# Matrix-memory mixer: the two halves of the partitions both filled with chunks, narrow products alternated over the array, and two pairs of output banks

## What is computed

```python
def step(carry, inp):                       # one chunk of 64 tokens, each head and direction
    c_mat, n_vec, m = carry
    qb, kb, vb, li, lf = inp
    b = jnp.cumsum(lf, -1)
    dmat = jnp.where(tri, b[..., :, None] - b[..., None, :] + li[..., None, :], -jnp.inf)
    m_inter = b + m[..., None]
    m_t = jnp.maximum(m_inter, jnp.max(dmat, -1))
    s = jnp.einsum('zhtd,zhsd->zhts', qb, kb) * jnp.exp(dmat - m_t[..., None])
    inter = jnp.exp(m_inter - m_t)
    num = inter[..., None] * jnp.einsum('zhtd,zhde->zhte', qb, c_mat) + jnp.einsum('zhts,zhse->zhte', s, vb)
    den = inter * jnp.einsum('zhtd,zhd->zht', qb, n_vec) + jnp.sum(s, -1)
    h_out = num / jnp.maximum(jnp.abs(den), jnp.exp(-m_t))[..., None]
    b_last = b[..., -1]
    g = b_last[..., None] - b + li
    m_new = jnp.maximum(b_last + m, jnp.max(g, -1))
    wts, decay = jnp.exp(g - m_new[..., None]), jnp.exp(b_last + m - m_new)
    c_mat = decay[..., None, None] * c_mat + jnp.einsum('zhs,zhsd,zhse->zhde', wts, kb, vb)
    n_vec = decay[..., None] * n_vec + jnp.einsum('zhs,zhsd->zhd', wts, kb)
    return (c_mat, n_vec, m_new), h_out
```

## Time and profile before

| what | value |
|---|---|
| three executions | 2066.82, 2070.66, 2060.62 us; median 2066.82 us |
| span of the profiled execution | 2063.7 us; its own time is not listed apart from the three |
| PE busy | 1966.4 us, 95% of the span |
| DVE, ACT, POOL busy | 732.5, 407.5, 39.4 us |
| DMA | 512.93 MB, mean 249 GB/s |
| chain that ended last | PE 87%, DMA 5%, DVE 4%, issue 2%, ACT 2% |

### The profile page before, as it was taken

How to read it: one execution, slowest core, us unless ns; L and a number is a source line. 1 busy time by engine, 2 the same in 40 slices (tenths; PEclk the granted TensorE clock), 3 DMA queues, 4 the chain that set the end, 5 groups by cost and what they waited for, 6 DMA issues and landing times.

```text
span 2063.7 us, 34642 instructions
## 1 busy us (share of the span) xinstructions
PE 1966.4 (95%) x15286; PEld 1321.4 (64%) x15286; DVE 732.5 (35%) x1578; ACT 407.5 (20%) x804; POOL 39.4 (2%) x41
## 2 busy tenths in 40 slices
PE   6999988999999999999899999999998989999998
PEld 3554865887554455445475888888877876463564
DVE  2694589564311111111335255323673420010001
ACT  3200263322211111111235200003222120000001
POOL 0000211000000000000000000000000000000000
PEclk9999997799999999999999999999999999999999
DMA  9710006017799999999756369753300059999992
GB/s 366 255 41 0 1 1 229 20 42 285 302 430 426 429 428 427 426 431 429 291 220 245 132 226 376 275 206 131 126 19 2 1 225 361 413 409 407 412 401 97
DMA packets 162338, 512.93 MB, mean 249 GB/s; under 512 B 9070, under 2 KB 32413, under 8 KB 149533
## 3 DMA queue, kind: packets, MB, share of 16 engines
q1 hardware_dynamic: 146720, 481.18, 59.0%
q10 hardware_dynamic: 15485, 29.77, 3.9%
HBM read 509.88 MB, written 1.05 MB: 248 GB/s over the span
## 4 chain that ended last, share of the span: by engine, by line
PE 87%; DMA 5%; DVE 4%; issue 2%; ACT 2%; SPq 0%; DVEq 0%; POOL 0%; ACTq 0%; POOLq 0%
PE PS L389 26%; PE PS L2614 11%; PE PS L2638 5%; PE PS L2450 4%; PE PS L2529 3%; PE PS L2740 3%; PE PS L2540 3%; PE PS L2732 3%; DMA work<-in_moe_w_gate_up_dram 2%; PE PS L396 2%; DMA work<-in_w_ada_dram 2%; PE PS L3324 2%; PE PS L2744 2%; PE PS L2820 1%; PE PS L2159 1%
## 5 line engine op out<-in xcount | busy, mean ns | idle before, releaser
L389 PE MATMUL PS<-hT,work 128*128 128x256 f32 x1408 | 313.1, 382 | 0.0
L389 PEld LDWEIGHTS PS<-hT,work 128*128 128x128 f32 x1408 | 266.8, 191 | 42.2 <-issue 6.2
L2614 PE MATMUL PS<-work,sq 128*64 128x512 f32 x1024 | 222.6, 592 | 0.0
L389 PE MATMUL PS<-work 128*128 128x256 f32 (+1 forms) x544 | 177.1, 486 | 0.0
L2614 PEld LDWEIGHTS PS<-work,sq 128*64 128x64 f32 x1024 | 76.6, 137 | 143.2 <-issue 142.4
L389 PEld LDWEIGHTS PS<-work 128*128 128x128 f32 x544 | 103.0, 190 | 73.5 <-issue 66.0
L2638 PE MATMUL PS<-work 128*64 128x512 f32 x512 | 113.4, 595 | 10.1 <-issue 8.7
L2638 PEld LDWEIGHTS PS<-work 128*64 128x64 f32 x512 | 36.8, 137 | 76.4 <-issue 74.5
L2732 PE MATMUL PS<-work,sq 128*64 128x512 f32 (+1 forms) x384 | 78.8, 568 | 5.6 <-DMA work<-in_moe_w_gate_up_dram 5.6
L2682 DVE TENSOR_TENSOR work<-work,PS 128x64 f32<-128x64 f32 x128 | 18.2, 213 | 184.9 <-PE PS L2614 184.9
L2450 PE MATMUL PS<-work 128*128 128x256 f32 x352 | 76.3, 379 | 0.0
(11 more groups left out here) (662 smaller groups left out, 2628.9 us busy)
## 6 DMA issues: line engine op xcount, KB each, us to landing
work<-in_ex_gate_dram SPq DMA_DIRECT2D x32, 2048.0 KB, 12.6
work<-in_ex_up_dram SPq DMA_DIRECT2D x32, 2048.0 KB, 15.3
work<-in_ex_down_dram SPq DMA_DIRECT2D x32, 2048.0 KB, 11.4
work<-in_moe_w_gate_up_dram SPq DMA_DIRECT2D x32, 2048.0 KB, 13.3
work<-in_moe_w_down_dram SPq DMA_DIRECT2D x16, 2048.0 KB, 16.4
work<-in_ada_w_dram ACTq DMA_DIRECT2D x14, 2048.0 KB, 11.1
work<-in_moe_w_gate_up_dram SPq DMA_DIRECT2D x16, 1536.0 KB, 14.9
work<-in_ada_w_dram SPq DMA_DIRECT2D x10, 2048.0 KB, 11.0
```

The costliest lines, as they stand in the source:

```text
L389: ins = pe.matmul(outp, lhs, rhs, start=n == 0, stop=n == len(pairs) - 1, **kw)
L2614: ins = pe.matmul(PS[pair[m], 6 + j, :], xs[:, k, pair[m]], unit(U[name] + 3 * m + j, KT, F)[:, k, :], start=k == 0, stop=k == KT - 1)
```

## The change

Pairs of chunks (`cp`, 128 tokens) take the place of single chunks, on all 128 partitions: gate tokens, values, keys, decays, scores. Consecutive products go to different quarters or halves of PE's array by their partitions. The state keeps only the wanted blocks (even heads in the lower, odd heads in the upper partitions), so `Cst` is half as wide and needs no zeros. The two directions of a step always have chunks of opposite parity, so their outputs stand in opposite halves of one pair of banks, and successive steps take turns between banks 0, 1 and 2, 3; the state products take turns between banks 6, 7 and 4, 5. PE does the states of the next steps ahead of the outputs. In an output group PE waits once for its own records of the crossed products (`ml_num`, 2j + 1), as they go into the same places from other rows of the array. DVE gets eight small copies that bring floors and decays into the new order (`ml_floors_dve`). Waits elsewhere get new numbers only.

The core of the diff; lines of bodies that only lose are left out, they are in the listing above:

```diff
-    wtok = gates.take(NCH, R40)
-    gtok = gates.take(2, 4, R40)
+    wtok = gates.take(4, R40)
+    btok = gates.take(2, R40)
+    floors = gates.take(4, H)
+    decq = gates.take(4, 2, 4)
+    diag = gates.take(4, R40)
+    den, rden = gates.take(H), gates.take(H)
-    diag = ml.take(4, R40)
-    decb = ml.take(4, R40)
-    vt = ml.take(NCH, H, E1)
-    Cst = ml.take(4, 2, 8 * E1).rearrange("p j d (b q h e) -> p j d b q h e", b=2, q=2, h=2)
+    vt = ml.take(4, H, E1)
+    Cst = ml.take(4, 2, 4 * E1)
-    kwl = ml.take(2, 3, H * C)
-    Em = ml.take(8, H, C)
-    hs = ml.take(4, H * C)
-    den, rden = ml.take(H), ml.take(H)
+    kwl = ml.take(2, 2, H * C)
+    Em = ml.take(2, 2, H * C).rearrange("p c d (h t) -> p c d h t", t=C)
+    hs = ml.take(2, H * C)
...
-        pool.memset(vt[0:C, :, :, C:E1], 1.0)
-        pool.memset(Cst.rearrange("p j d b q h e -> p (j d b q h e)"), 0.0)
+        pool.memset(vt[:, :, :, C:E1], 1.0)
...
+        for g, (t, t0, n) in enumerate(((a_, N, 2), (wts, 0, 4), (einvm, 0, 2))):
+            for cp in range(n):
+                at = ML_SMALL[g] + cp * R40
+                pe.transpose(PS[:, 3, at:at + R40], t[0:R40, t0 + cp * P:t0 + (cp + 1) * P], i40)
...
         for d, rows in enumerate((nD, b_)):
-            if d:
-                pe.wait_ge(S["gate_rows"], 1)
-            for b in range(4):
-                for k in range(2):
-                    ins = pe.matmul(PS[0:C, 4 * (1 - d) + b, k * N:(k + 1) * N], pick[:, d * H + 2 * b + k, :], rows[:, N:],
-                                    start=True, stop=True)
+            by_half = rows[:, N:].rearrange("p (c r t) -> p r c t", r=2, t=C)
+            for b in range(2):
+                for k in range(4):
+                    for r in range(2):
+                        ins = pe.matmul(PS[half(r), 4 + 2 * d + b, k * P:(k + 1) * P].rearrange("p (c t) -> p c t", t=C),
+                                        pick[:, d * H + 4 * b + k, :], by_half[:, r], start=True, stop=True)
                 ins.then_inc(S["ml_e"], 1)
...
+        dve.tensor_copy(btok, ml_small(0, 2))
+        dve.tensor_copy(wtok, ml_small(1, 4)).then_inc(S["gate_rows"], 1)
...
+    def ml_floors_dve():
+
+        for r in range(2):
+            for d in range(2):
+                at = slice(3 - r, None, -2) if d else slice(r, None, 2)
+                dve.tensor_copy(floors[half(r), at, :].rearrange("p c (b q) -> p c b q", b=2),
+                                ml_small(2, 2)[half(r), :, gate_rows[d]].rearrange("p c (q b) -> p c b q", b=2))
+        for b in range(2):
+            for d in range(2):
+                at = slice(None, None, -1) if d else slice(None)
+                ins = dve.tensor_copy(decq[both(b), at, d, :],
+                                      ml_small(3, 4)[both(b), :, gate_rows[d]].rearrange("p c (q b) -> p b c q", b=2)[:, b])
+        ins.then_inc(S["gate_rows"], 1)
...
+        def turn(cp):
+            if cp >= 2:
+                pe.wait_ge(S["ml_kw"], cp - 1)
             for p in range(4):
+                ins = pe.transpose(PS[:, cp % 2, p * P:(p + 1) * P], k1[:, p, cp * P:(cp + 1) * P], ident)
             ins.then_inc(S["keys_turned"], 1)
         turn(0)
         turn(1)
+        for cp in range(4):
+            pe.wait_ge(S["gate_rows"], 1 + cp + 1)
+            for p in range(4):
+                ins = pe.transpose(PS[:, 4 + cp, p * P:(p + 1) * P], mv[:, p, cp * P:(cp + 1) * P], ident)
+            ins.then_inc(S["ml_vt"], 1)
+        pe.wait_ge(S["gate_rows"], 6)
+        for cp in range(2):
+            for h in range(H):
+                for c in (2 * cp, 2 * cp + 1):
+                    at = cp * 4 * C + (h // 2) * C
+                    ins = pe.matmul(PS[half(c), 2 + h % 2, at:at + C], k1[half(h), h // 2, N + c * C:N + (c + 1) * C],
+                                    q1[half(h), h // 2, c * C:(c + 1) * C], start=True, stop=True)
+        ins.then_inc(S["ml_sc"], 1)
+        pe.wait_ge(S["ml_ve"], 4)
+        for cp in range(2):
+            pe.wait_ge(S["ml_kw"], cp + 1)
             for d in range(2):
+                for h in range(H):
+                    p = h // 2
+                    ins = pe.matmul(PS[half(h), 4 + d, p * E1:(p + 1) * E1], kwc[:, cp, d, h * C:(h + 1) * C], vt[:, cp, h, :],
+                                    start=cp == 0 and p == 0, stop=cp == 1, skip_group_check=True)
+            turn(cp + 2)
+        ins.then_inc(S["ml_st"], 1)
...
+        for cp in range(4):
+            dve.wait_ge(S["keys_turned"], cp + 1)
+            for d in range(2):
+                dst = kwc[:, cp, d] if cp < 2 else kwl[:, cp - 2, d]
+                ins = dve.tensor_tensor(dst.rearrange("p (h e) -> p h e", h=H), PS[:, cp % 2, :].rearrange("p (h e) -> p h e", h=H),
+                                        along(wtok[:, cp, gate_rows[d]], C), ALU.mult)
             ins.then_inc(S["ml_kw"], 1)
+            if cp == 1:
+                ml_scores_dve()
...
+    def state_banks(j):
+
+        return slice(6, 8) if j % 2 == 0 else slice(4, 6)
     def ml_first_state_act():
+        act.wait_ge(S["ml_st"], 1)
+        act.activation(Cst[:, 0], PS[:, 4:6, 0:4 * E1], ACT.Copy).then_inc(S["ml_step"], 1)
+
+    def ml_state_pe(j):
+
+        if j == 0:
+            pe.wait_ge(S["ml_kw"], 4)
+        else:
+            pe.wait_ge(S["ml_step"], j)
+        for h in range(H):
+            for d in range(2):
+                c, p = ORDER[d][4 + j] - 4, h // 2
+                ins = pe.matmul(PS[half(h), state_banks(j).start + d, p * E1:(p + 1) * E1],
+                                kwl[half(c), c // 2, d, h * C:(h + 1) * C], vt[half(c), 2 + c // 2, h, :], start=p == 0,
+                                stop=True, skip_group_check=True)
+        ins.then_inc(S["ml_st"], 1)
     def ml_next_state_dve(j):
+        quads = lambda t: t.rearrange("p d (q e) -> p d q e", e=E1)
         dve.wait_ge(S["ml_step"], j + 1)
+        dv.link(dve.tensor_tensor(quads(Cst[:, j + 1]), quads(Cst[:, j]), along(decq[:, j], E1), ALU.mult))
+        dve.wait_ge(S["ml_st"], 2 + j)
+        dve.tensor_tensor(Cst[:, j + 1], Cst[:, j + 1], PS[:, state_banks(j), 0:4 * E1], ALU.add).then_inc(S["ml_step"], 1)
...
+    def ml_scores_dve():
+        dve.wait_ge(S["ml_exp"], 4)
+        dve.wait_ge(S["ml_sc"], 1)
+        for cp in range(2):
+            sc = PS[:, 2:4, cp * 4 * C:(cp + 1) * 4 * C].rearrange("p b (a t) -> p b a t", t=C)
+            for d in range(2):
+                e = Em[:, cp, d].rearrange("p (a b) t -> p b a t", b=2)
                 dve.tensor_tensor(e, e, sc, ALU.mult).then_inc(S["ml_p"], 1)
...
+    def ml_out_banks(j):
+
+        return slice(2 * (j % 2), 2 * (j % 2) + 2)
+
+    def ml_out_pe(j):
+
+        pe.wait_ge(S["ml_step"], j + 1)
+        if j == 0:
             pe.wait_ge(S["ml_args"], 5)
+        if j >= 2:
+            pe.wait_ge(S["chunk_out"], j - 1)
+        cs = [ORDER[d][4 + j] - 4 for d in range(2)]
+
+        def at(d, h):
+            return PS[half(cs[d]), ml_out_banks(j).start + h % 2, (h // 2) * E1:(h // 2 + 1) * E1]
+
+        crossed = lambda k: [(d, 2 * k + 1 - cs[d] % 2) for d in range(2)]
+        straight = lambda k: [(d, 2 * k + cs[d] % 2) for d in range(2)]
+
+        def from_state(d, h):
+            return pe.matmul(at(d, h), qs[half(h), d, h // 2, cs[d] * C:(cs[d] + 1) * C],
+                             Cst[half(h), j, d, (h // 2) * E1:(h // 2 + 1) * E1], start=h < 2, stop=False, skip_group_check=True)
+
+        def from_chunk(d, h):
+            return pe.matmul(at(d, h), Em[half(cs[d]), cs[d] // 2, d, h, :], vt[half(cs[d]), 2 + cs[d] // 2, h, :], start=False,
+                             stop=True, skip_group_check=True)
+
+        for k in range(4):
+            for d, h in crossed(k):
+                ins = from_state(d, h)
+            if k == 3:
+                ins.then_inc(S["ml_num"], 1)
+            for d, h in straight(k):
+                from_state(d, h)
+        for k in range(2):
+            for d, h in straight(k):
+                from_chunk(d, h)
+        pe.wait_ge(S["ml_num"], 2 * j + 1)
+        for k in range(2):
+            for d, h in crossed(k) + straight(2 + k):
+                from_chunk(d, h)
+        for k in range(2, 4):
+            for d, h in crossed(k):
+                ins = from_chunk(d, h)
         ins.then_inc(S["ml_num"], 1)
...
+    def ml_out_of_step_dve(j):
+        dve.wait_ge(S["ml_num"], 2 * j + 2)
+        hz = PS[:, ml_out_banks(j), 0:4 * E1].rearrange("p b (q e) -> p b q e", e=E1)
+        two = lambda t: t.rearrange("p (b q) -> p b q", b=2)
+        dv.link(dve.tensor_tensor(two(den), hz[:, :, :, C], two(floors[:, j]), ALU.max))
+        dv.link(dve.scalar_tensor_tensor(out=two(den), in0=hz[:, :, :, C], scalar=-1.0, in1=two(den), op0=ALU.mult, op1=ALU.max))
+        dv.link(dve.reciprocal(rden, den))
+        dst = hs[:, min(j, 3 - j), :]
+        o = (dst if j < 2 else kw2.rearrange("p h e -> p (h e)")).rearrange("p (q b e) -> p b q e", b=2, e=C)
```

(65 more changed lines are left out.)

161 lines of the change are left out of this document (20 added, 141 removed).

## The result

The changed kernel takes 2040.1 us (median of four runs, 2039.7 to 2042.9), the kernel before beside it 2068.3 us (2060.6 to 2070.7): ratio 0.988, 95% interval 0.986 to 0.990. 2038 us were forecast, with a range of 2030 to 2048; the kernel is faster by more than 0.5%. Measured twice more it took 2041.9 us (ratio 0.988, 0.985 to 0.991) and 2040.4 us (0.988, 0.985 to 0.991).

The account below looks back on a forecast made before the run. PE was taken to bound the matrix-memory part; 14.8 us from its first part and 13.7 from its four steps gave 28.5 us, a span of 2035.3 us, plus 3.1 to the median: 2038 us, range 2030 to 2048.

Parts of the forecast that it names:

- What comes after hangs on the lora start: First `rw_lora` products, 278.44 us before: if PE reaches them earlier by x, the kernel should end earlier by x.
- PE sets the end of this part: Matrix-memory part, 220.8 to 278.4 us: PE is the bound, with only short waits for DVE uncovered.
- Part A: Start to end of queries, 220.8 to 251.5 us: PE work sums to 15.65 us, ending 14.8 us earlier.
- selecting: Selecting products on PE: 64 records on alternate column halves at 59 ns, 3.8 us for 7.05 before.
- Part B: The four steps, 251.5 to 278.44 us: PE work sums to 13.1 us; gain 13.7 us.
- the 0.15 us for own records: Outputs of each step: PE's wait for its own records, taken as 0.15 us, bounds 0 and 0.5 us.
- The price of 20 ns: Cost per record of products over all four quarters of PE's array, from L1997: 0.63 us / 32.
- The rule against it: Outputs from the chunk: row halves sharing a bank might serialise, 63 ns for 34, costing 3.7 us.
- Covers: Work hidden behind other engines: DVE's outputs end about 252 us, ACT's lora copy 254.3, POOL's L1640 253.7.
- The sum: Whole kernel: 28.5 us earlier at the lora products, span 2063.7 - 28.4 = 2035.3 us.
- The dips there could cost some 4 us more or less: PE's tail, 283 to 400 us: clock dips in another phase, some 4 us either way, included in the range.
- the 3.1 us from span to median: Whole kernel: the runs' median stands 3.1 us above the span, taking 2035.3 us to 2038.4 us.

Follow-up runs that it names:

- e2: Changed kernel with DVE's biases, keys and scores in two instructions of 64 partitions for one of 128, PE unchanged: 2053.7 us, ratio 0.993.
- e4: Changed kernel with outputs from the chunk reordered, neighbouring products from different row halves writing different partitions of one bank: 2042.9 us in one run.
- e1: Changed kernel with only PE's narrow products reordered, four in a row on the same part of the array: 2047.9 us, ratio 0.991.
- e3: Changed kernel with one pair of output banks, each step waiting for DVE's reading of the step before: 2044.2 us, ratio 0.989.
- e5: Changed kernel with the queries' weights in banks of their own, without the wait for DVE's keys: 2037.3 us in one run, 2043.1 us repeated.
- e8: Changed kernel with 16 tiny products added on PE ahead of the gate tokens: 2036.5 us, ratio 0.985.
- e9: e5 with 22 tiny products added on PE ahead of the gate tokens: 2035.6 us, ratio 0.985.

## Why the prediction was right

- **What comes after hangs on the lora start.** Right for 1200 us: 29.1 us at the lora products, 30.7 and 30.1 us at the next two marks, for 28.5. "PE sets the end of this part" was right of the kernel before; in part A of the changed one it is DVE.
- **Part A.** 15.65 us were summed and 0.3 us of waiting added; it took 236.63 - 220.98 = 15.65 us with 0.55 us of waiting. Terms: gate tokens 0.94 for 0.85; selecting 3.64 for 3.8; 32 transposes 3.85 for 4.1; scores 1.09 for 1.3; context states 2.17 for 2.1; queries 3.4 for 3.5. The eight small copies took 1.06 us on DVE (0.133 each) for 1.0. The step that was named too lightly is the wait: DVE ended its last keys at 234.65 us, as worked out (234.8), but the sum calls PE the bound, and the chain and e2 show DVE there, with PE at its heels.
- **Part B.** It took 12.7 us, waits included, for 13.1 and 0.2 of waiting. States 1.7 for 1.9 and outputs 6.45 (4 x 1.61) for 7.6, in which the 0.15 us for own records didn't show in any of the four. The price of 20 ns was too high by its method: it divides the distance to the next group by 32, and behind L1997 comes a group of another shape. Its 32 records take 0.69 us in all, as those of L1440 do (0.65 to 0.70); followed by their own kind of group, they cost 15 to 18 ns. Prices too high and waits too short made up for each other: given back were 0.31 us for the queries (0.2 forecast) and 0.66 us ahead of output 2, forecast to be just in time (242.2 against 242.5): DVE's reads ended at 242.40 us, but the faster PE stood ready at 241.88 us. DVE's times hit to 0.3 us throughout: state 1 239.7 (239.4), output 1 245.1 (245.0), output 2 247.2 (247.1). The 0.3 us come from the decay beside POOL (1.07 us for the 0.70 of the sum), on the path to that last wait.
- **The rule against it.** By it the outputs from the chunk would take 63 ns; they take 33 ns, and 34 ns where e4 provokes the conflict. The Trainium skill, TensorEngine Tiling, "Restrictions and Gotchas", says that different row tiles cannot access the same PSUM bank simultaneously; neither trace agrees, for products of 64*64 on the two diagonal quarters that write different partitions. For products over all four quarters the floor of about 25 ns from start to start that the Trainium skill, TensorE: Matmul & The Clock Gate, "Wait — 56ns, not 53.3ns?", states doesn't show: 64 records of the scores start within 1.09 us, 17 ns apart.
- **Covers.** POOL ran from 248.55 us for 5.36 us (248.3 forecast), and the lora copies of ACT ended at 253.79 us (254.3). What I had left out is that some of DVE's instructions are slower beside POOL:

```profile
246.51 0.69 DVE L1478 TENSOR_TENSOR work<-work 128x512 f32<-128x512 f32 x1
...
250.98 1.75 DVE L1478 TENSOR_TENSOR work<-work 128x512 f32<-128x512 f32 x1
...
252.66 1.28 DVE L1710 TENSOR_SCALAR tmp<-param_cols 128x4 f32<-128x4 f32 x1
```

The second add lies beside POOL's L1648, the first doesn't. This used up all of the slack forecast for DVE (done at 252 us against ACT's 254.3): DVE ends L1710 at 253.94 us, after ACT, and starts L1713 at 253.98 us, up to 0.2 us later than ACT would have let it.
- **The sum** failed behind the part. The span came out 25.2 us shorter, for 28.4. "The dips there could cost some 4 us more or less" was said of the stretch to 400 us, which kept all of the gain and more; the loss came in the gated-delta stretch and took 6.8 us: about 5 us of low clock and 2 us of pauses. The working had no term for the place of a product in PE's stream, and none for the clock there.
- **Luck.** That 2038 us and 2040.1 us lie 2.1 us apart is in part luck. The faster terms (0.6 us at the lora products), 1.6 us on the way to the inverse and 1.9 us after the stretch made up for over half of the loss. And the 3.1 us from span to median were no fixed distance: the profiled execution of the changed kernel takes 2040.28 us with a span of 2038.5, 1.8 us more, as in every run here. By that the execution profiled before took an estimated 2065.5 us; the other 1.3 us are its distance from the median and nothing of the kernel.

## What to carry to other kernels

Two chunks on the two halves of the partitions pay twice, in DVE's count of instructions and in overlap on PE; but the overlap is got by the order of issue, and runs of four or eight on one part lose much of it (41 and 52 ns for 17 in the scores). When PE's part of a stretch is halved, work out DVE's beside it to the tenth of a microsecond: the next bound, and which banks must be free when, came out of that sum. Ask of every cover on GpSimd which DVE instruction runs beside it: 0.4 us on the path went there, and an edit worth as much was lost to it. And compare the whole timeline, not the changed part: add up its pauses and its low clock before putting a late loss down to the change.

## What the hardware showed beyond the forecast

- Records over four quarters of the array cost 15 to 18 ns from group to group (L1328, L1371, L1440), where they took 20 ns in L1997 with a group of another shape behind it.
- Of DVE's instructions that touch no PS, three took longer beside POOL: the decay 1.07 or 1.48 us for 0.70 (L1380, ending 0.55 to 0.56 us after POOL's L1646), the add 1.75 for 0.69 (L1478), and a 128x4 product 1.28 us, ending with POOL's L1648. Others did not: those with an operand in PS (L1475, 0.69 us), a reciprocal (L1472, 0.20 us), and a 64x512 add of the kernel before, within the time that the trace gives to POOL's L1640. Which property decides stays open:

```profile
279.95 0.68 DVE L1473 TENSOR_TENSOR work<-work 64x512 f32<-64x512 f32 x1
```
- PE's idle times without a wait lie at every 256th place of its stream and nowhere else: 67 of 67 in fourteen profiles.
- DVE pieces that alternate between the two halves of the partitions follow at 0.70 us, pieces on the same partitions at 0.62 us (L1348, 4 in 2.48).
- In six of the twelve profiles with the changed part (e1, e2, e3, e5 again, e8, e9) the clock stood at its lower level for a while between 220 and 227 us and cost 1.7 us; the selecting products took 5.22 to 5.38 us for 3.71 (6.10 in e1, with its order). The same kernel (e5) had it in one run and not in another, so no edit brings it by itself; neither profile of the kernel before has it. What brings it is open.
